# Scores of 64-feature heads on all 128 rows: zero-padded keys, gates in the padding, a mask on 128 columns

## What is computed

```python
# kind "m": 8 heads of 64, causal (the one block of 256 keys is the query's own)
s_own = jnp.einsum('bhqd,bhkd->bhqk', qc, k_own).astype(jnp.float32) * scale
s_own = jnp.where(causal, s_own, -jnp.inf)

# kind "f": 8 heads of 64, causal, with cumulated log gates
cum = jnp.cumsum(log_f, axis=-1)
scores = (jnp.einsum('bhqd,bhkd->bhqk', qc, k).astype(jnp.float32) * scale
          + cq[..., None] - cum[:, :, None, :])
scores = jnp.where(causal, scores, -jnp.inf)

# second model, layer 1: 8 heads, each with two components of 64
sc = jnp.einsum('bhcqd,bhckd->bhcqk', qb, k).astype(jnp.float32) * scale
p = masked_softmax(sc, mask)
attn = p[:, :, 0] - lmb * p[:, :, 1]
```

## Time and profile before

| | |
|---|---|
| median of 3 runs | 2006.52 us (2005.86 to 2010.3) |
| the profiled execution | 2011.58 us, its span 2009.8 us |
| PE busy | 1891.4 us, 94% of the span |
| DVE, ACT, POOL busy | 75%, 60%, 8% |
| HBM read | 509 MB, 254 GB/s over the span |
| chain that ended last | PE 73%, DVE 17%, DMA 4%, ACT 3% |
| mean granted PE clock | 0.975 of 2.4 GHz |

### The profile page before, as it was taken

One profiled execution on the slowest core, in us unless ns is written; L12 is line 12 of the kernel. 1 busy time (PEld: TensorE's weight loads), 2 busy tenths in 40 slices (PEclk: granted clock), 3 DMA queues, 4 the chain that ended last, 5 costly groups with the idle time before them and its releaser, 6 DMA issues.

```text
span 2009.8 us, 22518 instructions
## 1 busy us (share of the span) xinstructions
PE 1891.4 (94%) x9235; PEld 1554.0 (77%) x9235; DVE 1499.4 (75%) x1433; ACT 1211.5 (60%) x1243; POOL 159.8 (8%) x121
## 2 busy tenths in 40 slices
PE   5999999999998999989969999999999999999994
PEld 4778777888987778877758887888778887888873
DVE  4745456544689754467678889898999989898996
ACT  4554445433563344335546778876887778777873
POOL 2401010000133220032120000000000000000000
PEclk9999999999999999989988999999999999999997
DMA  8433334544532455444256999999999999999991
GB/s 280 148 134 137 127 126 167 209 174 145 191 140 84 147 199 199 146 146 169 84 188 230 375 362 403 400 388 358 377 409 398 375 356 404 409 387 359 379 410 63
DMA packets 154318, 511.62 MB, mean 255 GB/s; under 512 B 4335, under 2 KB 8673, under 8 KB 139873
## 3 DMA queue, kind: packets, MB, share of 16 engines
q1 hardware_dynamic: 151888, 502.91, 66.4%
q0 software_dynamic: 1424, 4.59, 0.8%
q10 hardware_dynamic: 896, 2.62, 0.3%
HBM read 509.05 MB, written 1.05 MB: 254 GB/s over the span
## 4 chain that ended last, share of the span: by engine, by line
PE 73%; DVE 17%; DMA 4%; ACT 3%; issue 2%; POOL 0%; DVEq 0%; SPq 0%; ACTq 0%; POOLq 0%
PE PS L430 20%; PE PS L432 19%; PE PS L431 19%; DVE WLB L1797 6%; DVE WLX L1797 5%; DMA ring<-in_moe_w_down 3%; PE PS L1097 2%; PE PS L1098 1%; ACT WHB L1223 1%; PE PS L877 1%; PE PS L1030 1%; DMA ring<-in_w_mem_kv 1%; PE PS L596 1%; PE PS L941 1%; DVE AR L2182 1%
## 5 line engine op out<-in xcount | busy, mean ns | idle before, releaser
L1223 ACT ACTIVATE WHB<-ring 128x2048 fp32r<-128x2048 f32 (+1 forms) x344 | 534.1, 1561 | 346.3 <-PE PS L432 311.9
L1797 DVE TENSOR_TENSOR WLB<-ring,WHB 128x2048 fp32r<-128x2048 f32 (+1 forms) x344 | 646.1, 1893 | 129.4 <-ACT WHB L1223 128.8
L1797 DVE TENSOR_TENSOR WLX<-ring,WHX 128x2048 fp32r<-128x2048 f32 (+1 forms) x216 | 468.1, 2192 | 51.9 <-ACT WHX L1223 51.9
L1223 ACT ACTIVATE WHX<-ring 128x2048 fp32r<-128x2048 f32 (+1 forms) x216 | 393.6, 1837 | 159.4 <-PE PS L432 135.8
L430 PE MATMUL PS<-WHB,XH 128*128 128x512 f32 (+1 forms) x640 | 257.6, 402 | 12.5 <-DVE XL L1846 6.8
L432 PE MATMUL PS<-WHB,XL 128*128 128x512 f32 (+1 forms) x640 | 250.6, 392 | 0.0
L431 PE MATMUL PS<-WLB,XH 128*128 128x512 f32 (+1 forms) x640 | 250.1, 391 | 0.0
L2629 POOL TENSOR_TENSOR SM<-SM,MH 128x8 f32<-128x8 f32 (+3 forms) x28 | 38.6, 1384 | 1440.5 <-DVE SM L1810 1440.5
L430 PEld LDWEIGHTS PS<-WHB,XH 128*128 128x128 f32 x640 | 122.6, 192 | 38.6 <-issue 11.9
L432 PEld LDWEIGHTS PS<-WHB,XL 128*128 128x128 f32 x640 | 122.1, 191 | 26.1
L431 PEld LDWEIGHTS PS<-WLB,XH 128*128 128x128 f32 x640 | 122.5, 191 | 23.3
(11 more groups left out here) (398 smaller groups left out, 3532.8 us busy)
## 6 DMA issues: line engine op xcount, KB each, us to landing
ring<-in_moe_w_gate SPq DMA_DIRECT2D x56, 2048.0 KB, 10.3
ring<-in_moe_w_up SPq DMA_DIRECT2D x56, 2048.0 KB, 10.7
ring<-in_moe_w_down SPq DMA_DIRECT2D x56, 2048.0 KB, 10.7
ring<-in_w_in SPq DMA_DIRECT2D x13, 2048.0 KB, 8.0
ring<-in_hg_w_in SPq DMA_DIRECT2D x8, 2048.0 KB, 8.4
ring<-in_da_w_in SPq DMA_DIRECT2D x6, 2048.0 KB, 7.9
ring<-in_w_gate SPq DMA_DIRECT2D x5, 2048.0 KB, 9.0
ring<-in_w_up SPq DMA_DIRECT2D x5, 2048.0 KB, 7.7
```

What stands on the lines that cost most here:

```text
L1223: e.activation(hi, src, ACT.Copy).then_inc(s_hi, 1)
L1797: e.tensor_tensor(lo, src, hi.bitcast(F32), ALU.subtract).then_inc(s_lo, 1)
```

## The change

`IDB` times `CSB` now adds the mask on the last 128 columns alone, in all three kinds; `CSB` is only 128 wide. Keys of even heads are held in one tile whose rows 64 to 127 hold padding, keys of odd heads in another whose rows 0 to 63 do (`KH["km"]`, `KH["kf"]`, late `KD[0]`, `KD[1]`), and a score is one matmul over all 128 rows. For "m" and the late heads the padding of the keys is zero and q stays as it was. For "f" the keys' padding holds the cumulated gates in its first 8 rows (the sums are made for rows 0 to 7 and 64 to 71 by `LGP`, zero elsewhere), and q is held in two tiles too, whose padding holds a one in the head's row and zeros elsewhere; L600 goes. ACT copies each such tile with two activations of 64 rows. POOL fills the padding: memsets, and copies of the identity's columns and of `NCT` into whole tiles, before ACT writes the other half. The late keys have room for four heads each, so dk1's copy waits until head 3 is scored.

```diff
@@ -139,7 +139,7 @@
-CSB = sb("CSB", [128, 256], BF16)
+CSB = sb("CSB", [128, 128], BF16)
...
@@ -334,9 +334,13 @@
-SEL = ar(AR1, 16384, 8, 128)[0:8]
+LGP = AR1[:, 17536:17792].rearrange("p (a n) -> p a n", a=2)
...
-NCT = VS[0:8, 0:256]
+NCT = VS[:, 0:256]
+KH = {"km": (ar(AR1, 7168, 4, S), ar(AR1, 9216, 4, S)), "kf": (ar(AR1, 8192, 4, S), ar(AR1, 9216, 4, S)),
+      "qf": (ar(AR1, 10240, 4, S), ar(AR1, 11264, 4, S))}
@@ -385,7 +389,7 @@
-FZ, FA1, FA2, FA3, LG = (sm(16).rearrange("p (a h) -> p a h", a=2) for _ in range(5))
+FZ, FA1, FA2, FA3 = (sm(16).rearrange("p (a h) -> p a h", a=2) for _ in range(4))
@@ -581,24 +585,20 @@
-            q_, k_ = QT[qn], QT[kn]
...
-                    t = e.matmul(PS[2][:, 256 * qt:256 * qt + 256], q_[:, h, 128 * qt:128 * qt + 128], k_[:, h, :], start=True, stop=True)
+                    t = e.matmul(PS[2][:, 256 * qt:256 * qt + 256], QT[qn][:, h, 128 * qt:128 * qt + 128], QT[kn][:, h, :], start=True, stop=True)
...
-                o, j = 64 * (h % 2), h // 2
-                pe.wait_ge(s_const, 3)
+                j = h // 2
+                q_, k_ = QT[qn] if a == "m" else KH[qn][h % 2], KH[kn][h % 2]
+                pe.wait_ge(s_const, 2)
...
-                    e.matmul(PS[2][:, a0:a1], q_[o:o + 64, j, 128 * qt:128 * qt + 128], k_[o:o + 64, j, 0:n], start=True, stop=False)
-                    if a == "f":
-                        pe.wait_ge(s_sel, 1)
-                        pe.wait_ge(*banks.out["cum"])
-                        e.matmul(PS[2][:, a0:a1], SEL[:, h, :], NCT[:, 0:n], start=False, stop=False)
-                    t = e.matmul(PS[2][:, a0:a1], IDB[:, :], CSB[:, 256 - n:256], start=False, stop=True)
+                    e.matmul(PS[2][:, a0:a1], q_[:, j, 128 * qt:128 * qt + 128], k_[:, j, 0:n], start=True, stop=False)
+                    t = e.matmul(PS[2][:, a1 - 128:a1], IDB[:, :], CSB[:, :], start=False, stop=True)
@@ -617,18 +617,18 @@
-            narrow(3, "fg", "x", W8[0], W8[1], NCT)
+            narrow(3, "fg", "x", W8[0], W8[1], NCT[0:8])
...
-            e.matmul(PS[3][0:8, 0:128], LG[:, 0, :], triu, start=True, stop=True)
-            e.matmul(PS[3][0:8, 128:256], LG[:, 0, :], ONE, start=True, stop=False)
-            e.matmul(PS[3][0:8, 128:256], LG[:, 1, :], triu, start=False, stop=True)
-            e.matmul(PS[3][:, 256:264], triu, LG[:, 0, :], start=True, stop=True)
-            e.matmul(PS[3][:, 264:272], ONE, LG[:, 0, :], start=True, stop=False)
-            e.matmul(PS[3][:, 264:272], triu, LG[:, 1, :], start=False, stop=True).then_inc(banks.put("cum", 3), 1)
+            e.matmul(PS[3][:, 0:128], LGP[:, 0, :], triu, start=True, stop=True)
+            e.matmul(PS[3][:, 128:256], LGP[:, 0, :], ONE, start=True, stop=False)
+            e.matmul(PS[3][:, 128:256], LGP[:, 1, :], triu, start=False, stop=True)
+            e.matmul(PS[3][:, 256:264], triu, LGP[:, 0, 0:8], start=True, stop=True)
+            e.matmul(PS[3][:, 264:272], ONE, LGP[:, 0, 0:8], start=True, stop=False)
+            e.matmul(PS[3][:, 264:272], triu, LGP[:, 1, 0:8], start=False, stop=True).then_inc(banks.put("cum", 3), 1)
@@ -935,11 +935,10 @@
-            o = 64 * c
...
-                e.matmul(PS[b][:, a0:a1], QD[o:o + 64, h, 128 * qt:128 * qt + 128], KD[o:o + 64, h, 0:n], start=True, stop=False)
-                t = e.matmul(PS[b][:, a0:a1], IDB[:, :], CSB[:, 256 - n:256], start=False, stop=True)
+                e.matmul(PS[b][:, a0:a1], QD[:, h, 128 * qt:128 * qt + 128], KD[c][:, h % 4, 0:n], start=True, stop=False)
+                t = e.matmul(PS[b][:, a1 - 128:a1], IDB[:, :], CSB[:, :], start=False, stop=True)
@@ -1294,7 +1293,24 @@
-        dst, src = QT[n][:, :, 128 * tt:128 * tt + 128], PS[3][:, :].rearrange("p (j n) -> p j n", j=4)
+        src = PS[3][:, :].rearrange("p (j n) -> p j n", j=4)
+        if n in KH:
+            if n == "km":
+                a.wait_ge(s_kz, 2)
+            else:
+                a.wait_ge(s_sel, 2 if n == "qf" else 4)
+            for x in range(2):
+                o = slice(64 * x, 64 * x + 64)
+                to = KH[n][x][o, :, 128 * tt:128 * tt + 128]
+                if n in GAIN_COL:
+                    c = GAIN_COL[n]
+                    t = e.activation(to, src[o], ACT.Copy, scale=VT[o, c:c + 1])
+                else:
+                    t = e.activation(to, src[o], ACT.Copy)
+            t.then_inc(banks.out["t", n, tt][0], 1)
+            return
+        dst = QT[n][:, :, 128 * tt:128 * tt + 128]
@@ -1577,9 +1593,18 @@
-        dst = (QD if n[1] == "q" else KD)[:, 4 * int(n[2]):4 * int(n[2]) + 4, 128 * tt:128 * tt + 128]
+        i, cs = int(n[2]), slice(128 * tt, 128 * tt + 128)
+        src = PS[2 + tt][:, :].rearrange("p (j n) -> p j n", j=4)
...
-        e.activation(dst, PS[2 + tt][:, :].rearrange("p (j n) -> p j n", j=4), ACT.Copy).then_inc(banks.out["t", n, tt][0], 1)
+        if n[1] == "q":
+            e.activation(QD[:, 4 * i:4 * i + 4, cs], src, ACT.Copy).then_inc(banks.out["t", n, tt][0], 1)
+        else:
+            a.wait_ge(*(banks.full["dsc", 3, 1] if i else (s_kd, 2)))
+            for c in range(2):
+                o = slice(64 * c, 64 * c + 64)
+                t = e.activation(KD[c][o, :, cs], src[o], ACT.Copy)
+            t.then_inc(banks.out["t", n, tt][0], 1)
@@ -1882,9 +1907,6 @@
-            if k == "f" and h == 0:
-                v.wait_ge(s_sq, 12)
-                e.tensor_copy(SEL, CT[0:8, C_ID:C_ID + 8].unsqueeze(2).to_broadcast([8, 8, 128])).then_inc(s_sel, 1)
@@ -1914,7 +1936,7 @@
-            e.tensor_copy(NCT, PS[3][0:8, 0:256]).then_inc(banks.out["fg", 0][0], 1)
+            e.tensor_copy(NCT[0:8], PS[3][0:8, 0:256]).then_inc(banks.out["fg", 0][0], 1)
@@ -1922,10 +1944,12 @@
-            e.tensor_tensor(LG, FA1, FA3, ALU.subtract).then_inc(s_lg, 1)
+            v.wait_ge(s_pset, 4)
+            e.tensor_tensor(LGP[:, :, 0:8], FA1, FA3, ALU.subtract)
+            e.tensor_tensor(LGP[:, :, 64:72], FA1, FA3, ALU.subtract).then_inc(s_lg, 1)
...
-            e.tensor_scalar(NCT, PS[3][0:8, 0:256], -8.0, None, ALU.mult)
+            e.tensor_scalar(NCT, PS[3][:, 0:256], -8.0, None, ALU.mult)
@@ -1980,8 +2004,7 @@
-    e.memset(CSB[:, 0:128], 0.0).then_inc(s_const, 1)
-    e.tensor_copy(CSB[:, 128:256], CT[:, C_CAUS:C_CAUS + 128]).then_inc(s_const, 1)
+    e.tensor_copy(CSB[:, :], CT[:, C_CAUS:C_CAUS + 128]).then_inc(s_const, 1)
@@ -2670,18 +2693,36 @@
+    e.memset(LGP, 0.0).then_inc(s_pset, 1)
...
+    p.wait_ge(*banks.full["cols", "x", 3])
+    for x in range(2):
+        e.memset(KH["km"][x], 0.0).then_inc(s_kz, 1)
...
+    def cumulated(x):
+        e.tensor_copy(KH["kf"][x], NCT.unsqueeze(1).to_broadcast([128, 4, S])).then_inc(s_sel, 1)
+    p.wait_ge(s_tab, 16)
+    p.wait_ge(*banks.full["sc", "c", 3])
+    for x in range(2):
+        c = C_ID + 64 * (1 - x)
+        ones = CT[:, c:c + 8].rearrange("p (j x) -> p j x", x=2)[:, :, x:x + 1].to_broadcast([128, 4, S])
+        e.tensor_copy(KH["qf"][x], ones).then_inc(s_sel, 1)
+    p.wait_ge(*banks.out["cum"])
+    cumulated(0)
...
+    p.wait_ge(*banks.full["sc", "m", 7])
+    cumulated(1)
@@ -2749,6 +2790,9 @@
+    p.wait_ge(s_used, FIRST["E"])
+    for c in range(2):
+        e.memset(KD[c], 0.0).then_inc(s_kd, 1)
@@ -2843,7 +2887,9 @@
-QD, KD = ar(AR3, 3840, 8, S), ar(AR3, 5888, 8, S)
+QD = ar(AR3, 3840, 8, S)
+KD = [ar(AR3, 5888 + 1024 * c, 4, S) for c in range(2)]
```

More of the change, by code:

```diff
@@ L202, in build @@
         s_tab, s_x, s_mem, s_vec, s_bc, s_ln, s_outd, s_lvt, s_pset = (sem(n) for n in ("s_tab", "s_x", "s_mem", "s_vec", "s_bc", "s_ln", "s_outd", "s_lvt", "s_pset"))
-        s_tab2 = sem("s_tab2")
+        s_tab2, s_kz, s_kd = sem("s_tab2"), sem("s_kz"), sem("s_kd")
         s_hid, s_hth, s_htl, s_sgt, s_ub, s_perm = sem("s_hid"), sem("s_hth"), sem("s_htl"), sem("s_sgt"), sem("s_ub"), sem("s_perm")
```

## The result

The changed kernel takes 1986.5 us in the median of 4 runs (1984.6 to 1987.2), against 2008.4 us in 4 runs of the kernel before. The ratio is 0.9892 with a 95% interval of 0.9878 to 0.9906: 1.1% faster, 19 to 25 us. The forecast was 25 us and 1981.5 us, with a range of 1976.5 to 1994. Of the 5.0 us between 1981.5 and 1986.5, 1.9 us are the kernel before, which stood at 2006.5 us in the forecast and at 2008.4 us here.

What follows compares the result with a forecast made beforehand. PE was taken to set the pace in both attention stretches. Gains of 4.7 ("m"), 13.1 ("f") and 7.2 us (late) sum to 25.0 us, taking the 2006.5 us median to 1981.5 us, range 1976.5 to 1994.

Steps and rivals of the forecast that it cites:

- What bounds: Both attention stretches: PE sets the pace, so a microsecond less PE work shortens the span equally unless a wait takes it.
- The change of rows: Scores and gate matmuls in heads: each whose number of rows differs from the next one's pays 0.20 us more, whatever its width.
- rival A: Masks behind scores: the 0.20 us belongs to the type change too; gain 13.0 us, time 1993.5 us; chance 0.14.
- terms of 0.09 us for a mask: Each block's two masks on 128 columns: 0.09 us each, bounds 0.06 and 0.16, within a block of 0.83 us.
- What takes some of it back: Late attention: a longer third-head wait and longer dk1 copies cut the late gain from 9.4 to 7.2 us.
- (a): Third late head: DVE's and ACT's order stays, so the second head's 1.18 us only lengthens PE's wait.
- (b): dk1's copy out of PSUM: two more activations at 0.53 us each lengthen PE's wait by 1.07 us.
- (c): Late part of the sum: the longer waits priced at 1.2 and 1.1 us, leaving 7.2 us gain.
- The edits at nothing: Other doubled copies, POOL's fills and memsets, DVE edits, larger gate sums: costed at nothing; copy covers 0.2 and 0.3 us.
- rival C: POOL's last fill of kf delays ACT's copy, PE starves: slower, just above 2010 us; chance 0.03 with similar cases.
- The rule that I set aside: Late heads: array tiles work in parallel, so components share 1.42 us and padding costs 1.9 us; rejected from the rows.
- Rival B: Last four "f" heads: softmax waits replace shorter scores; gain 18.4 us, time 1988.1 us if all lost; chance 0.05.

Runs made afterwards that it cites:

- long_wait: Kernel before plus one ACT activation copying 1024 constants ahead of the second late head's exponentials; ratio 0.9999, late stretch 65.1 us.
- late_undone: Changed kernel with its late part taken back (64-row scores, full-width masks, one copy per unit); ratio 0.9924, late stretch 65.0 us.
- turn3_later: Changed kernel with only the turning of the fourth late head's P one quarter later; ratio 0.9885, late stretch 55.2 us.
- score2_later: Changed kernel with only the third late head's score and its mixing one quarter later; ratio 0.9877, late stretch 54.7 us.
- late_grouped: Kernel before with each late head's two component scores side by side on 64 rows, then their masks; ratio 0.9969, late stretch 55.8 us.

## Why the prediction was right in sign and size, and where its steps failed

**What bounds.** Right. Early, 8 x (1.42 - 0.88) + 8 x (2.47 - 0.87) = 17.1 us of shorter heads came out as 174.0 - 155.8 = 18.2 us of the stretch, against a forecast of 17.8. That these two are so near is partly luck, since the profile of before had one thing more in that stretch. At the end of a head of "f", at 269.9 us, the granted clock fell to the lower level for 3.4 us, though PE had waited for nothing for longer than 0.3 us:

```profile
270.00:273.00 3.00, 3.00 (x9) 2.32 (x8) 1.91 (x5) 0.91 (x4) 0.00 (x0) 0.50 0.03 5
```

The four profiles with the early code of before all have this, each at the end of a head of "f" (two such stretches in `long_wait`, with 175.5 us early; one in each of the others, with 174.0). The seven with the changed early code have none between 120 and 500 us (155.8 or 155.9 us early in each). So the change also did away with a fall of the clock that had cost about 1.5 us; what in the 64-row and 8-row heads brings it about was not tested.

**The change of rows.** The price was right, and the type of the data costs nothing (rival A): the float32 score hands over to the bf16 mask in 0.22 us on 128 columns and in 0.49 us on 256, nearer to the forecast's 0.43 than to A's 0.63. The loads of the stationary tiles show where half of the 0.20 us lay. Before, the load for a 64-row score began with the score's own record at 206.63 us; after, it begins 0.14 us ahead of the record at 203.92, beside the matmul before it:

```profile
206.63 0.29 PEld L596 LDWEIGHTS PS<-AR 64*128 64x128 f32 x2 [0.36 <-issue]
```

```profile
203.78 0.33 PEld L600 LDWEIGHTS PS<-AR 128*128 128x128 f32 x2
```

No head of any run has two scores on the same 64 rows next to each other, apart from the two records of one. So it is not separated whether a change of the number of rows costs the 0.20 us or every float32 matmul on fewer than 128 rows does. For this kernel the sum is the same.

Instead of the forecast 0.83 us a block adds 0.88. Per mask, what follows the 128-column score is 0.05 us late, what follows the 256-column one adds 0.49 - 0.43 = 0.06 us to the score and 0.11 us behind it; so the terms of 0.09 us for a mask were a little small, and the dependence on width, from which I bounded them, did not show (the experiment with wide masks).

**What takes some of it back.** The two places were right, their price was not. (a) Third late head: forecast 1.2 us of longer wait, measured 2.42 - 1.34 = 1.1 us. (b) dk1's copies: forecast 1.1, measured 2.58 - 1.25 = 1.3 us, because four activations on 64 rows take 2.40 us and not four times 0.53:

```profile
952.61 2.40 ACT L1606 ACTIVATE AR<-PS 64x512 f32<-64x512 f32 x4
```

(c) The step that failed: the sum priced a wait at its length. With each of these waits the clock fell to half, where a projection step takes 957.47 - 957.04 = 0.43 us instead of 0.23, and the single moves put 1.5 and 1.7 us on that. The late part was forecast at 7.2 us and gave 2.7 (against 62.0) to 5.8 us (against the 65.1 of the same code in another profile). The 2.7 us add up: 8 x 1.08 = 8.6 us of shorter heads, less 2.4 us of longer waits, less 3.2 to 3.4 us of lower clock. That the whole came out only 3 us short of 25 is partly luck too: the kernel before lost to its own clock in most profiles, both early and late, and that loss was in no term of the sum.

```profile
957.04 0.63 PE L434 MATMUL PS<-WHB,XH 128*128 128x512 f32 x1
957.47 0.63 PE L435 MATMUL PS<-WLB,XH 128*128 128x512 f32 x1
```

**The edits at nothing.** These covers held, though thinly. kf's second copies ran from 202.36 to 203.73 us for a score at 203.92; dk0's four ended at 915.44 + 2.40 = 917.84 for one at 917.94. POOL's last fill of kf took 1.03 us and was done at 192.52, 2.7 us ahead of ACT at 195.26 (rival C's place):

```profile
202.36 1.37 ACT L1308 ACTIVATE AR<-PS,VT 64x512 f32<-64x512 f32 x2
203.92 0.38 PE L600 MATMUL PS<-AR 128*128 128x128 f32 x2
...
191.49 1.03 POOL L2711 COPY AR<-VS 128x1024 f32<-128x1024 f32 x1
```

**The rule that I set aside.** The prediction held against the Trainium skill's page "TensorEngine Tiling (Array Packing)", section Key Properties, that both components together took 2.84 us. That was a misreading: they were never neighbours, a mask on 128 rows stood between them. As neighbours they take the time of one (0.43 and 0.64 us for two), and the prediction's list of rivals should have had that case. The page's rule agrees with that trace, and its rival time, a late head that is dearer padded than paired, is real by 0.16 us a head; the estimate of 1.42 us for a pair was too low; it came to 1.60 us, with the four masks one behind the other (0.21 us for the two on 128 columns).

**Rival B** did not come in "f" (no wait for exponentials there). **The rest of the 24.4 us** of the two profiled spans is not the change: the expert stage, whose code is the same, took 767.7 us before and 761.7 after, from the first to the last record of one line (L1097 before, L1096 after), and 760 to 765 in the nine other kernels. The median ratio, 1.1%, is the better measure: some 22 us. The profiles put 18 of them early and 3 to 6 late; the whole time of `late_undone`, the early part alone, puts 15 early. Neither tells the split more closely than by 3 us.

## What to carry to other kernels

Read what a matmul costs from its start to its neighbour's start, and look at whether the number of rows changes between them: here each float32 matmul on 64 or 8 rows, followed by one on another number, cost 0.20 us more than on full rows, 0.4 of the 1.42 us that a head of "m" added. Either pad to full rows or put the half-row ones side by side; and when PE gets shorter ahead of a wait, price the wait at its length and what the clock does behind it, then see whether a step can be moved so that there is no wait at all: two moved steps gave 8 us more than the change alone.

## What the runs showed of the hardware that was not expected

Behind a wait of 2.4 to 3.5 us in the late attention the granted clock fell every time it was profiled (two waits in the changed kernel, two with wide masks, one each in `turn3_later`, `score2_later` and `late_grouped`); behind the one of 1.3 us ahead of the third head it fell in two profiles of three (`late_undone`, `long_wait`, not the kernel before); in the three kernels without such waits it never fell there. The same late code with the same wait thus ran 3 us differently from one execution to another.

The length of the wait alone does not decide it. Ahead of the late heads, in code that is the same in all kernels, PE waits once for 2.6 us, and the clock fell there in six profiles of eleven and stayed in five. This is one of the five, the kernel before:

```profile
906.17 0.47 PE L430 MATMUL PS<-WHB,XH 128*128 128x512 f32 x1 [2.63 <-DVE XL L1846]
```

```profile
905.00:911.00 6.00, 4.83 (x21) 4.02 (x22) 4.15 (x9) 4.85 (x7) 0.20 (x1) 1.00 0.83 312
```

And behind heads of "f" on 64 and 8 rows it fell without such a wait, as told above. What decides it was not found.

Two float32 matmuls on rows 0 to 63 and 64 to 127, into two banks, run in the time of one (0.43 us on 128 columns, against 0.42 for one). A bf16 mask of 128 or 256 columns between a float32 score and the next projection costs the same (a head of "m" adds 0.88 us with either). An activation on 64 partitions and 512 elements takes 0.6 us (2.40 for four), no less than one on 128 (1.07 us for two).
